# Block 2's three norms: where their squares are added, where the residual lies, and the order of the first tiles

## The reference, cut to what matters

```python
x = h + jax.nn.sigmoid(h @ ple_w_gate[i]) * (p[i] @ ple_w_proj[i])      # end of each layer of block 1
...
def rms_norm_2(x, g):
    xf = x.astype(jnp.float32)
    y = xf * lax.rsqrt(jnp.mean(xf * xf, axis=-1, keepdims=True) + EPS)
    return (y * g.astype(jnp.float32)).astype(x.dtype)
...
h = jnp.concatenate([pad, meta, x], axis=1)
h = h + hybrid_mixer(rms_norm_2(h, attn_norm_g[layer]), w_in[layer], forget_b[layer], ...)
h = h + conv_ffn(rms_norm_2(h, ffn_norm_g[layer]), w_up[layer], conv_w[layer], ...)
return rms_norm_2(h, final_norm_g)[:, PREFIX:]
```

## Time and profile before

| | |
|---|---|
| runs | 3, median 2371.61 us (2370.99 to 2375.19) |
| profiled execution | span 2367.5 us from its first to its last instruction; the page gives no other time of it |
| PE, PEld (weight loads) | 97%, 79% of the span |
| DVE, ACT, POOL | 37%, 38%, 51% |
| chain of work that ended last | PE 85%, POOL 6%, ACT 5%, issue 2%, DVE 2% |
| mean granted clock of PE | 0.991 of full speed |

### The profile page before, as it was taken

One profiled execution on the slowest core, in us unless ns is written; L12 is line 12 of the kernel. 1 busy time (PEld: TensorE's weight loads), 2 busy tenths in 40 slices (PEclk: granted clock), 3 DMA queues, 4 the chain that ended last, 5 costly groups with the idle time before them and its releaser, 6 DMA issues.

```text
span 2367.5 us, 31663 instructions
## 1 busy us (share of the span) xinstructions
PE 2290.4 (97%) x12399; PEld 1858.9 (79%) x12399; DVE 879.5 (37%) x1437; ACT 891.6 (38%) x1258; POOL 1203.8 (51%) x1059
## 2 busy tenths in 40 slices
PE   8999998899999989999989999998999999999998
PEld 6777777688888777777768888876888888889897
DVE  4556654421221422666432122143554323313132
ACT  4344342624224443555362332345233324323233
POOL 4565765444444465888644444444312334545452
PEclk9999999999999999999999999999999999999999
DMA  5222222132222231212222223223212112233321
GB/s 152 72 65 78 72 72 70 64 100 96 89 92 99 74 97 54 63 55 67 85 81 89 89 90 105 89 71 99 73 38 54 54 54 72 90 89 97 98 81 62
DMA packets 237433, 188.94 MB, mean 80 GB/s; under 512 B 9279, under 2 KB 228860, under 8 KB 237196
## 3 DMA queue, kind: packets, MB, share of 16 engines
q1 hardware_dynamic: 233616, 183.66, 25.1%
q10 hardware_dynamic: 3708, 3.79, 0.5%
HBM read 185.30 MB, written 2.10 MB: 79 GB/s over the span
## 4 chain that ended last, share of the span: by engine, by line
PE 85%; POOL 6%; ACT 5%; issue 2%; DVE 2%; DMA 0%; ACTq 0%; DVEq 0%; POOLq 0%
PE ps L2519 43%; PE ps L2722 11%; PE ps L1371 8%; PE ps L636 4%; PE ps L2609 2%; PE ps L2542 2%; POOL w_lo L1783 2%; POOL hdd L421 1%; POOL hdd L419 1%; PE ps L2584 1%; PE ps L2552 1%; PE ps L1338 1%; PE ps L1433 1%; PE ps L702 1%; ACT w_hi L1945 1%
## 5 line engine op out<-in xcount | busy, mean ns | idle before, releaser
L1783 POOL TENSOR_TENSOR w_lo<-raw,w_hi 128x512 fp32r<-128x512 f32 (+2 forms) x760 | 897.6, 1215 | 830.3 <-ACT w_hi L1945 829.7
L1945 ACT ACTIVATE w_hi<-raw 128x2048 fp32r<-128x2048 f32 (+2 forms) x190 | 330.0, 1738 | 516.7 <-PE ps L2519 362.5
L2519 PE MATMUL ps<-a_hi,w_hi 128*128 128x512 f32 (+1 forms) x912 | 293.4, 353 | 8.9 <-POOL a_lo L843 4.8
L2519 PE MATMUL ps<-b_hi,w_hi 128*128 128x512 f32 x752 | 296.2, 394 | 3.2 <-POOL w_lo L1783 3.2
L2519 PE MATMUL ps<-b_hi,w_lo 128*128 128x512 f32 x752 | 298.3, 397 | 0.0
L2519 PE MATMUL ps<-b_lo,w_hi 128*128 128x512 f32 x752 | 296.6, 394 | 0.0
L2519 PE MATMUL ps<-a_lo,w_hi 128*128 128x512 f32 (+1 forms) x912 | 293.7, 354 | 0.0
L2519 PE MATMUL ps<-a_hi,w_lo 128*128 128x512 f32 (+1 forms) x912 | 293.1, 353 | 0.0
L2519 PEld LDWEIGHTS ps<-a_hi,w_hi 128*128 128x128 f32 x912 | 162.3, 190 | 36.9 <-issue 11.1
L2519 PEld LDWEIGHTS ps<-a_hi,w_lo 128*128 128x128 f32 x912 | 161.2, 190 | 24.2
L2519 PEld LDWEIGHTS ps<-a_lo,w_hi 128*128 128x128 f32 x912 | 160.6, 190 | 24.2
(11 more groups left out here) (377 smaller groups left out, 4183.0 us busy)
## 6 DMA issues: line engine op xcount, KB each, us to landing
raw<-in_mlp_w_dram SPq DMA_DIRECT2D x128, 512.0 KB, 4.3
raw<-in_w_up_dram SPq DMA_DIRECT2D x44, 512.0 KB, 5.1
raw<-in_ssd_w_in_dram SPq DMA_DIRECT2D x40, 512.0 KB, 4.8
raw<-in_hgrn_w_in_dram SPq DMA_DIRECT2D x48, 256.0 KB, 3.2
raw<-in_w_in_dram SPq DMA_DIRECT2D x24, 512.0 KB, 5.0
raw<-in_ssd_w_out_dram SPq DMA_DIRECT2D x16, 512.0 KB, 4.2
raw<-in_w_down_dram SPq DMA_DIRECT2D x16, 512.0 KB, 3.9
raw<-in_ple_w_gate_dram SPq DMA_DIRECT2D x12, 512.0 KB, 4.0
```

The costliest lines, as they stand in the source:

```text
L1783: last = nc.gpsimd.tensor_tensor(w_lo[:, slot, piece], raw[:, slot, i * q:(i + 1) * q], w_hi[:, slot, piece].bitcast(F32), ALU.subtract)
L1945: nc.scalar.activation(w_hi[:, slot, at:at + n], raw[:, slot, 0:n], ACT.Copy).then_inc(whi_ready, 1)
L2519: last = nc.tensor.matmul(ps[:, b + s, 0:nn], w[:, k, m * P:(m + 1) * P], v[:, k, c0 + s * nn:c0 + (s + 1) * nn], start=(k == 0 and first) ...
```

## The change

- In the gate stages the order of DVE and ACT changes: DVE adds tile m directly behind its multiply, and ACT takes what follows a tile directly behind that tile's sigmoid (`after(m)`). In layer 1 DVE writes the sum to `res` at its final place, behind the meta columns, and ACT squares it there (`squared`) in place of the copy; block 1 uses `res` at this offset everywhere.
- The meta tokens are turned and copied earlier, in layer 1's MLP.
- The squares of the tiles 1 to 6 are added by DVE into slot 0 of `sq` (`add_square`), which waits for ACT's square of the tile. PE does two products with that sum and two with the square of tile 7. This holds for all three norms; in the second and third `add_square` stands behind the eviction of the tile.
- The first two tiles of the input projection are done together, first all products with a_hi, then those with a_lo. The same holds for the first chunk of the FFN.
- The forget gate's products go to four column groups of 32, two rounds, after the high parts; DVE copies the rows, and PE adds them up by two products.
- Some buffers move.

```diff
@@ block2_act
-            def rms2_act(there, before, last=False):
-                if not last:
+            def rms2_act(i, before):
+                if i:
                     act.preload_act_table_set("natural_log_exp_and_others")
-                for k in range(KD):
-                    if not last:
-                        act.wait_ge(there, before + k + 1)
...
-                    act.wait_ge(sq_used, sq_at(k - 3 if k >= 4 else 0))
-                    nc.scalar.activation(sq[:, k % 4, :], res[:, k, :], ACT.Square).then_inc(ln_sq, 1)
+                    for k in range(KD):
+                        act.wait_ge(free_dve, before + k + 1)
+                        square2(i, k)
...
             next_cut(16, 4)
             tile.add(4)
-            rms2_act(free_dve, FD_PROJ + KD)
+            rms2_act(1, FD_PROJ + KD)
@@ block2_dve
+            dve.wait_ge(ff_rows, 1)
+            nc.vector.tensor_copy(two(fp[:, 0, :]), pair(2)).then_inc(ff_kept, 1)
             dve.wait_ge(fl_ready, 1)
...
                 ins.then_inc(free_dve, 1)
+                if t >= 32:
+                    add_square(1, t - 32)
...
+                    if last:
+                        add_square(2, m)
@@ block2_pe
-            def rms2_pe():
-                for k in range(KD):
-                    pe.wait_ge(ln_sq, sq_at(1))
-                    for s in range(2):
-                        last = nc.tensor.matmul(bank[4 + s][:, 0:H2], ones, sq[:, k % 4, s * H2:(s + 1) * H2],
-                                                start=(k == 0), stop=(k == KD - 1))
-                    last.then_inc(sq_used, 1)
-                    sq_at.add()
+            def rms2_pe(i):
+                b = 4 if i else 3
+                pe.wait_ge(q_sum, 6 * (i + 1))
+                for s in range(2):
+                    nc.tensor.matmul(bank[b + s][:, 0:H2], ones, sq[:, 0, s * H2:(s + 1) * H2], start=True, stop=False)
+                pe.wait_ge(ln_sq, sq_at(KD))
+                for s in range(2):
+                    last = nc.tensor.matmul(bank[b + s][:, 0:H2], ones, sq[:, sq_slot(KD - 1), s * H2:(s + 1) * H2],
+                                            start=False, stop=True)
+                last.then_inc(sq_used, KD)
+                sq_at.add(KD)
...
+            def forget_rows():
+                pe.wait_ge(s_ff, 32)
+                pe.wait_ge(ff_pad, 1)
+                pe.wait_ge(xc_ready, 8 * KD)
+                for j in range(2):
+                    for s in range(2):
+                        for g in range(4):
+                            last = nc.tensor.matmul(bank[2 + s][HEADS * g:HEADS * (g + 1), 0:H2], wff[:, 4 * j + g, :],
+                                                    xc[:, 4 * j + g, s * H2:(s + 1) * H2], start=(j == 0), stop=(j == 1))
+                last.then_inc(ff_rows, 1)
+            def forget_sums():
+                pe.wait_ge(ff_kept, 1)
                 for s in range(2):
+                    last = nc.tensor.matmul(bank[2 + s][0:8, 0:H2], pick[:, 0:8].bitcast(F32),
+                                            fp[:, 0, s * H2:(s + 1) * H2], start=True, stop=True)
+                last.then_inc(ff_done, 1)
@@ slices: tiles 0 and 1 together
-                for t in range(24):
+                pe.wait_ge(wlo_ready, chunk(3))
...
+                for n in range(2 * KD):
+                    k = n if n < KD else (n + 4) % KD
+                    if n < KD:
+                        pe.wait_ge(ahi_ready, 6 * KD + (k + 1))
+                    elif k >= LN_LO:
+                        pe.wait_ge(alo_dve, 5 * (KD - LN_LO) + (k - LN_LO + 1))
+                    else:
+                        pe.wait_ge(alo_ready, ALO[6] + (k + 1))
+                    for m in range(2):
+                        for w, v in ((wh, a_hi), (wl, a_hi)) if n < KD else ((wh, a_lo),):
...
+                    yield
+                chunk.add()
+                for t in range(2, 24):
...
-            fill(16)
+            fill(8)
+            forget_rows()
+            fill(5)
+            forget_sums()
+            fill(3)
             pe.wait_ge(s_constb, 16)
-            fill(3)
+            fill(4)
+            pe.wait_ge(fl_ready, 1)
             logits(0)
             logits(1)
-            fill(5)
+            fill(4)
             turn_v(0)
...
                     chunk_mm(j % 2, KD, 256, a, (fa, fd), geo=((b, 12, 258, 2), (b + 2, META, T, 1)), far=mark if j == 0 else None,
-                             ready=(alo_ready, ALO[7]) if j == 0 else None,
-                             late=(alo_dve, 6 * (KD - LN_LO)) if j == 0 else None)
+                             opened=(7 * KD, ALO[7], 6 * (KD - LN_LO)) if j == 0 else None)
@@ scalar queue
+            def square2(i, k):
+                if k >= 4:
+                    act.wait_ge(q_sum, 6 * i + (k - 3))
+                else:
+                    act.wait_ge(sq_used, sq_at())
+                nc.scalar.activation(sq[:, sq_slot(k), :], res[:, k, :], ACT.Square).then_inc(ln_sq, 1)
+            def squared(k):
+                if k == 0:
+                    act.wait_ge(meta_ready, 1)
+                if k == KD - 1:
+                    act.preload_act_table_set("natural_log_exp_and_others")
                 act.wait_ge(xc_ready, pub(1))
-                nc.scalar.activation(res[:, k, META:], xc[:, k, 0:T], ACT.Copy).then_inc(res_ready, 1)
+                square2(0, k)
                 pub.add()
...
-                        if m:
-                            after(m - 1)
+                        after(m)
...
-            publish(KD - 1)
...
-            ple_act(to_res)
+            ple_act(squared)
@@ vector queue
+            def add_square(i, k):
+                if 0 < k < KD - 1:
+                    dve.wait_ge(ln_sq, SQ2 + i * KD + (k + 1))
+                    dve.wait_ge(q_sum, 6 * i + (k - 1))
+                    nc.vector.tensor_tensor(sq[:, 0, :], sq[:, 0, :], sq[:, sq_slot(k), :], ALU.add).then_inc(q_sum, 1)
...
-                for m in range(KD + 1):
-                    if m < KD:
-                        dve.wait_ge(free_act, fa0 + (m + 1))
...
-                    if m >= 1:
-                        dve.wait_ge(free_dve, fd(-1 if m < KD else 0))
-                        nc.vector.tensor_tensor(xc[:, m - 1, 0:T], xc[:, m - 1, 0:T], res[:, m - 1, 0:T],
-                                                ALU.add).then_inc(xc_ready, 1)
+                for m in range(KD):
+                    dve.wait_ge(free_act, fa0 + (m + 1))
...
+                    dve.wait_ge(free_dve, fd())
+                    nc.vector.tensor_tensor(res[:, m, META:] if i else xc[:, m, 0:T], xc[:, m, 0:T], res[:, m, META:],
+                                            ALU.add).then_inc(xc_ready, 1)
+                    if i:
+                        add_square(0, m)
```

More of the change, by code:

```diff
@@ L925, in publish2 @@
                     pub.add()
[L928 to L932, removed]
+            rms2_act(0, None)
             publish2()
@@ L938, in block2_act @@
             act.wait_ge(ff_done, 1)
-            own.did(nc.scalar.activation(two(fz[:]), pair(4, 8), ACT.Identity, bias=fb[:]))
+            own.did(nc.scalar.activation(two(fz[:]), pair(2, 8), ACT.Identity, bias=fb[:]))
             own.wait()
@@ L1102, in block2_act, with block2_dve @@
                 nc.scalar.activation(otok[:, n % 4], bank[n % 6], ACT.Copy).then_inc(ot_ready, 1)
-        def block2_dve(dve, tile, fd, own, pub, b_at):
+        def block2_dve(dve, tile, fd, own, pub, b_at, add_square):
             def rms2_dve(i, col):
@@ L1344, in block2_pe @@
-            pe.wait_ge(free_dve, fd(-3))
-            for k in range(KD):
-                last = nc.tensor.transpose(bank[7][:, k * META:(k + 1) * META], mtok[:, k * P:(k + 1) * P],
-                                           ident[0:META, 0:META])
-            last.then_inc(meta_done, 1)
-            rms2_pe()
+            def rms2_pe(i):
[9 more added lines that the diff above has]
+                sq_at.add(KD)
@@ L1647, in block2_pe @@
             b_at.add(4)
[L1648 removed]
+            rms2_pe(1)
             def ffn(nt):
@@ L2032, in p_act @@
                     nc.scalar.activation(phi[:, k], bank[p_bank[k]], ACT.Copy).then_inc(p_hi, 1)
+                if i:
+                    act.wait_ge(meta_done, 1)
+                    nc.scalar.activation(res[:, :, 0:META], bank[5][:, 0:KD * META].rearrange("p (k n) -> p k n", k=KD),
+                                         ACT.Copy).then_inc(meta_ready, 1)
             def ple_act(after):
@@ L2212, in _ @@
             publish_ln(3, 1.0)
-            ple_act(to_res)
-            block2_act(act, chunk, tile, fa, own, pub, b_at, sq_at, cut_hi)
+            ple_act(squared)
+            block2_act(act, chunk, tile, fa, own, pub, b_at, sq_at, cut_hi, square2)
         @block.vector
@@ L2239, in add_to_res @@
                     dve.wait_ge(tile_done, tile(1))
```

(13 more changed lines are left out.)

91 lines of the change are left out of this document (43 added, 48 removed).

## The result

The change made the kernel slower: 2382.64 us, median of 4 runs (2381.38 to 2384.85), against 2371.96 (2370.99 to 2375.19); ratio 1.0046, 95% interval 1.0034 to 1.0058. The prediction was 2381.3 us, and slower with a chance of 0.64. The profiled execution of after took 2384.85 us with a span of 2383.1, so 1.75 lie around the span. If as much lay around the span of before, that execution took 2369.3. Between the profiles lie therefore 15.6 us, between the medians 10.7: one profile is a short execution and the other a long one, and small sums of stages are read with that in mind.

A forecast was written before the change was run, and what follows sets the result against it. TensorE, busy 97% of the span, was taken as the bound. Terms of +3.55 us without the clock and +6.15 for it brought the profiled span from 2367.5 to 2377.2; with 4.1 around it 2381.3 us, range 2370 to 2389.

The forecast's parts named there:

- Gate stages: Ends of layers 0 and 1: ACT's cut comes later behind waits for DVE, costing +3.5 and +2.75 us.
- The terms of 0.25: Gate stages: the add waits for its multiply, +0.25 us each at gate 7's weights (both layers) and layer 0's following stage.
- the clock behind gate 4: Layer 0: half clock behind PE's new gap of 3.4 us before gate 4, costing 1.7 us.
- Layer 1's clock: Layer 1's gate stage: the gap of 2.85 us before gate 4 was to bring no half-clock loss.
- Entry: Block 2: DVE's norm starts 5.8 us earlier, but PE waits 9.8 us before the logits; net -0.1 us.
- the 1.1 for a slow last add: Entry of block 2: DVE's last add of squares falls into POOL's cut, +1.1 us before the norm.
- the one short stretch assumed: Entry norm of block 2: half clock around two gaps of 3 us, put at 0.85 us (half).
- Tile 36: Block 2's output projection: PE waits 6.0 to 7.1 us for a bank, 6.5 taken, as DVE waits for ACT's squares.
- Norms: Less time from last eviction to norm: -4.75 us behind block 2's projection, -4.6 us at the last norm.
- FFN: First FFN tiles: earlier start against a later first eviction, between -1.0 and +1.4 us, taken as 0.
- The clock's share: Half clock behind new gaps in layer 0, entry norm, logits and projection: +6.15 us, bounds 0 and twice that.

The follow-up runs named there:

- e9: e8 with layer 0's gate stage put back as the change has it: 2360.49 us, ratio 0.9950 to the kernel before.
- e5: The changed kernel with ACT's cuts in both gate stages right behind their sigmoid, ahead of the copies or squares: 2374.89 us, ratio 1.0010.
- e1: The changed kernel with the old order of ACT's and DVE's work in layer 0's gate stage alone: 2382.38 us, ratio 1.0038.
- e3: The changed kernel with DVE's sums of squares in block 2's output projection moved behind later evictions: 2373.82 us, ratio 1.0007.
- e4: The changed kernel with DVE's eight memsets for the logits moved ahead of its wait for ACT's forget-gate logarithm: 2381.34 us, ratio 1.0037.
- e2: The changed kernel with the first two tiles of every FFN pass one after the other, as before: 2379.75 us, ratio 1.0030.
- e6: The changed kernel with PE's waits at gate 4 (both layers), entry norm and first logits filled with thrown-away products: 2378.34 us, ratio 1.0033.
- e12: e8 with the high-first pair of tiles kept in the FFN's first pass alone: 2354.06 us, ratio 0.9925 to the kernel before.
- e7: The kernel before with one part alone: the first two tiles of every FFN pass done high parts first: 2376.90 us, ratio 1.0025.
- e10: e8 with PE's three remaining waits at block 2's entry filled with thrown-away products: 2349.59 us, ratio 0.9898 to the kernel before.
- e8: The changed kernel with cuts first, old order of first FFN tiles, late sums in the projection and early memsets together: 2354.07 us, ratio 0.9923.

## Why the prediction was right, and where it was not

**Gate stages: right.** Cut 6.56 us behind sigmoid 0 (predicted 6.72), in layer 1 5.39 (5.72); PE's gaps 2.96 and 2.55 (3.4 and 2.85), released by POOL. The terms of 0.25 (two in layer 0, one in layer 1) were too high: the wait before gate 7 grew by 0.14 and 0.12, that before the HGRN by 0.02. What was taken for the clock behind gate 4, 1.7, was also a little high: PE worked 2.81 us at half rate there, which costs 1.4. e9 and e5 show that the cut behind the waits is the cause.

**Layer 1's clock: wrong.** "layer 1's 2.85 none": behind 2.55 us of waiting PE ran at half rate for 6.8 us in the profile of after, some 3 us lost (it worked 6.09 of the 6.70 shown), for 3.4 in those of e1, e3 and e4, and in that of e2 not at all. With the gap filled (e6) it did not fall.

**Entry: the mechanism right, the clock too small.** Norm 5.94 behind sigmoid 7 (6.6; the 1.1 for a slow last add did not come, it took 0.69), forget rows 1.99 (1.8, so the column groups do run side by side), wait 9.01 (9.8), 13.54 us from ACT's first step to the logits (14.0). But ACT's first step came 17.87 us after DVE's norm, not 14.6: the granted clock was 0.50 for 10.2 us instead of the one short stretch assumed, and the high parts took 10.6 us, not 7.8. This and layer 1's clock make up the +4.1 on the way to the logits.

**Tile 36: right.** 7.12 us (6.0 to 7.1). The add in front of the eviction that released it took 1.83 beside POOL's low parts, which ran from 1961.03 to 1966.43; the next add, behind them, took 0.71. The rule in the Trainium skill (page "SBUF — State Buffer", section "SBUF: two separate sides") gave 7.1 and agrees with this row. e3 shows the cause.

**Norms: right.** 4.07 us from the last eviction's start to DVE's norm (4.0 to 4.3), 2.61 to the last logarithm (2.5).

**FFN: the step that failed.** "both tiles now end together, so the first eviction starts later. Between -1.0 and +1.4; I take 0." About 0 holds for one pass (e12), but the edit stands in code that all three passes run, and the other two have no early start to set against it: with the half-rate stretch behind the second wait they cost 2.01 + 1.7 + 1.36, about 5 us. e7, with all three passes, measures +4.8.

**Sums.** That the forecast came within 1.3 us is partly luck: 5 us of the FFN were missing, layer 1's clock too, and terms that were too high made up for them; in the profiles, moreover, 1.6 us of the other rows lie ahead of gate 2 of layer 0, where nothing was forecast. The clock's share was put at 6.15; how much of it a run pays varies, as the profiles of e1 to e4 show, and what decides where it falls when PE does not stand still stays open.

## What to carry to other kernels

On an in-order engine, put the instruction that feeds the bottleneck (here the cut) ahead of any instruction that waits for another engine, even if both are ready in the same microsecond. When an edit stands in a loop body, count its cost once per pass, and ask in which passes its gain exists. And a gap of TensorE can cost more than its length (behind those here came 0 to 10.2 us at half rate): shorten it, or fill it with products that end before the awaited tile is there (those of e10 did not). Judge a single repair by its stage as well as by the time: here a part that no edit is aimed at differed by up to 4.4 us between executions.

## What the runs showed of the hardware

- The granted clock fell to 0.50 behind waits of 2.3 to 3.2 us in some executions and not in others of the same program part. At layer 1's gate 4 PE waited 2.55, 2.53, 2.50, 2.55 and 2.30 us in after and e1 to e4, and 6.8, 3.4, 0, 3.4 and 3.4 us at half rate followed. At layer 0's gate 4 waits of 2.96 (after) and 3.21 (e3) were followed by 3.4 us, waits of 3.04 (e2), 2.96 (e4) and 3.02 (e9) by none. With PE kept busy by products that are thrown away it stayed at 1.00 (e6, e10).
- It also fell where PE had not stood still: in e4 at 1834 us, behind products on 64 and 16 partitions. After has the same products and kept 1.00 there. In e4:

```profile
1831.52 1.77 PE L1570 MATMUL ps<-xc 64*128 64x512 f32 x4
1833.22 1.15 PE L1584 MATMUL ps<-rsm,rvt 16*128 16x264 f32 x4
1834.30 1.07 PE L1570 MATMUL ps<-xc 64*128 64x256 f32 x2
```

- Three of the undoings done alone moved the time by less than their own stage: e1 4.0 us in the stage and 0.3 in the median, e2 6.9 and 2.9, e4 7.7 and 1.3. The fourth, e3, did not: 8.0 and 8.8. Put back on the base of e8, layer 0's cuts cost 6.4 in the stage and 6.4 in the time, the memsets 6.5 and 3.1 to 4.6.
